# TensorE's program written out, and the first tile of a projection taken k by k

## What is computed

```python
def even_layer(h, ...):                     # layer 0
    z = rms_norm(h, pre_g) @ w_in           # 2048 x 6144
    u, pool_gate, q, k, v, attn_gate = jnp.split(z, EVEN_SPLITS, axis=-1)
    d, pool_state = multiscale_pool(u, pool_prev, positions)
    pool_out = grouped_linear(d, pool_w) * pool_scale
    o = diff_attn(rope(q), rope(k), v, lam) # prompt: causal; sample: paged cache
    o = rms_norm(o, subln_g) * (1.0 - LAMBDA_INIT)
    mix = jnp.concatenate([pool_out * silu(pool_gate), o * silu(attn_gate)], -1)
    return h + rms_norm(mix @ w_out, post_g)

def odd_layer(h, s0, ...):                  # layer 1
    z = rms_norm(h, pre_g) @ w_in           # 2048 x 6160
    q, k, v, gate, lr = jnp.split(z, ODD_SPLITS, axis=-1)
    g = log_sigmoid(lr @ wa2 + ba) / GLA_TAU
    o, st = gla_scan(q, k, v, g, s0, chunk) # gated linear attention, 4 heads
    o = rms_norm(o, norm_g) * silu(gate)
    return h + rms_norm(o @ w_out, post_g)
```

## Time and profile before

| | us |
|---|---|
| median of 3 runs | 2238.65 |
| lowest and highest run | 2235.77, 2240.67 |
| the profiled execution | 2231.26 |
| its span, from first to last instruction | 2229.1 |
| mean granted clock of TensorE | 0.949 of 2.4 GHz |

### The profile page before, as it was taken

One profiled execution on the slowest core, in us unless ns is written; L12 is line 12 of the kernel. 1 busy time (PEld: TensorE's weight loads), 2 busy tenths in 40 slices (PEclk: granted clock), 3 DMA queues, 4 the chain that ended last, 5 costly groups with the idle time before them and its releaser, 6 DMA issues.

```text
span 2229.1 us, 39746 instructions
## 1 busy us (share of the span) xinstructions
PE 2036.3 (91%) x15037; PEld 1873.0 (84%) x15037; DVE 813.0 (36%) x1402; ACT 644.5 (29%) x1158; POOL 816.2 (37%) x369
## 2 busy tenths in 40 slices
PE   4998898889889998899889999999999899969995
PEld 4987898789878887899879878987997799759995
DVE  4355236523652454300261444053315322550004
ACT  5132222222221221322233333333224232442122
POOL 1353236232622352645454212421332233144553
PEclk7999999999989999999999999999999899979997
DMA  6444234423442443433234342444244325433322
GB/s 199 150 132 135 79 110 119 133 77 117 124 119 74 120 131 112 136 94 89 69 104 115 114 142 77 114 130 136 68 120 148 113 67 147 146 126 95 94 75 77
DMA packets 357433, 252.49 MB, mean 113 GB/s; under 512 B 15135, under 2 KB 324784, under 8 KB 356720
## 3 DMA queue, kind: packets, MB, share of 16 engines
q1 hardware_dynamic: 316364, 186.75, 29.3%
q10 hardware_dynamic: 40900, 63.41, 8.4%
HBM read 213.61 MB, written 36.96 MB: 112 GB/s over the span
## 4 chain that ended last, share of the span: by engine, by line
PE 70%; issue 10%; POOL 6%; DVE 5%; SPq 3%; DMA 3%; ACT 2%; POOLq 0%; ACTq 0%; DVEq 0%
PE proj L983 57%; PE scratch L983 9%; PE score L983 3%; POOL wlo L554 3%; DMA qb<-q_sample_rows 2%; SPq L466 1%; SPq L458 1%; PE scratch L986 1%; POOL mix L608 1%; POOL kv L575 1%; DVE probw L1494 1%; DVE xlo L1344 1%; DVE ek L1724 1%; POOL mix L623 1%; DMA kv<-in_cache_v 0%
## 5 line engine op out<-in xcount | busy, mean ns | idle before, releaser
L983 PE MATMUL proj<-xhi,wlo 128*128 128x268 f32 x4128 | 1209.5, 293 | 68.7 <-DVE xlo L1342 27.8
L983 PE MATMUL proj<-xhi,whi 128*128 128x268 f32 x4128 | 1196.7, 290 | 11.0 <-issue 11.0
L983 PE MATMUL proj<-xlo,whi 128*128 128x268 f32 x4128 | 1197.6, 290 | 0.0
L554 POOL TENSOR_TENSOR wlo<-wraw,whi 128x1024 fp32r<-128x1024 f32 x258 | 624.1, 2429 | 1055.6 <-ACT whi L634 1055.5
L983 PEld LDWEIGHTS proj<-xhi,wlo 128*128 128x128 f32 x4128 | 793.9, 192 | 108.3 <-issue 90.9
L983 PEld LDWEIGHTS proj<-xlo,whi 128*128 128x128 f32 x4128 | 793.5, 192 | 1.0
L983 PEld LDWEIGHTS proj<-xhi,whi 128*128 128x128 f32 x4128 | 790.6, 192 | 0.0
L634 ACT ACTIVATE whi<-wraw 128x1024 fp32r<-128x1024 f32 x258 | 264.4, 1046 | 481.6 <-PE proj L983 353.0
L1332 DVE TENSOR_TENSOR tz<-proj,rstd 128x536 f32<-128x536 f32 x72 | 51.5, 716 | 390.6 <-PE proj L983 390.1
L1634 DVE TENSOR_SCALAR mix<-proj,cols 128x536 f32 x32 | 24.8, 776 | 348.8 <-ACT te L640 177.8
L575 POOL TENSOR_TENSOR kv<-kv,qb 128x1024 f32<-128x1024 f32 x32 | 78.4, 2455 | 108.5 <-DMA qb<-q_sample_rows 55.4
(11 more groups left out here) (260 smaller groups left out, 1808.1 us busy)
## 6 DMA issues: line engine op xcount, KB each, us to landing
wraw<-in_w_in SPq DMA_DIRECT2D x192, 512.0 KB, 4.0
wraw<-in_w_out SPq DMA_DIRECT2D x64, 512.0 KB, 3.9
kv<-in_cache_k SPq DMA_DIRECT2D x128, 128.0 KB, 2.4
kv<-in_cache_v SPq DMA_DIRECT2D x128, 128.0 KB, 2.5
sst<-in_state_gla ACTq DMA_DIRECT2D x32, 512.0 KB, 5.3
out<-sst ACTq DMA_DIRECT2D x32, 512.0 KB, 3.6
hbuf<-h_residual ACTq DMA_DIRECT2D x2, 4288.0 KB, 14.7
vb<-v_sample_rows ACTq DMA_DIRECT2D x32, 256.0 KB, 5.8
```

Of the source, the lines that this page charges most:

```text
L554: pool.tensor_tensor(wlo[:, slot, :, 0:width], wraw[:, kc, :, 0:width], whi[:, slot, :, 0:width].bitcast(F32), ALU.subtract).then_inc(s_lo, 1)
L983: return pe.matmul(out, lhsT, rhs, start=start, stop=stop, skip_group_check=True)
```

## The change

1. TensorE's three loops become Python loops, so that its program is written out in full, with constants as semaphore targets.
2. The first tile of "in0", "out0" and "out1" is done by a new function, `first_tile`: block by block, both halves of the columns, each block waiting for its own low part. The order of blocks is `X_ORDER`.
3. `lows` of GpSimd is removed, and its semaphore `s_xp`. VectorE makes all 16 lows of each stage in `x_lo`, which takes a stretch of the order; ScalarE's high parts are made in `x_hi`. In the last pair and the last head both are called in pieces between the other work. For that ScalarE's last pair and head, and VectorE's last head, are written out behind loops that are one pass shorter, and `s_mix` is raised once for each block or group that becomes complete.
4. TensorE's waits for the constants (`s_c0`) and the masks (`s_maskr`) move from before the first pair into the jobs that read them.

```diff
+X_ORDER = {"in0": list(range(KT)), "out0": [0, 1, 2, 3, 4, 5, 8, 9, 10, 11, 12, 13, 6, 14, 15, 7],
+           "in1": list(range(KT)), "out1": list(range(KT))}
...
             # GpSimd
-            lows("out0")
...
-            lows("out1")
...
             # ScalarE
+            def x_hi(stage, a, b):
+                for i in range(a, b):
+                    k = X_ORDER[stage][i]
+                    if i == 0:
+                        act.wait_ge(s_tile, (N_OUT0 if stage == "out0" else N_OUT1) + 2)
+                        act.wait_ge(*(free_d.at("pair", "PO11", PAIRS - 2) if stage == "out0" else (s_head, GH - 1)))
+                    if stage == "out0" and k == 6:
+                        act.wait_ge(*free_d.at("pair", "PO01", PAIRS - 1))
+                    if stage == "out0" and k in (14, 7):
+                        act.wait_ge(s_mix, 1 if k == 14 else 2)
+                    if stage == "out1" and k >= 12:
+                        act.wait_ge(s_mix, 3 + k - 12)
+                    act.activation(xhi[:, k, :], mix[:, k, :], ACT.Copy).then_inc(s_xhi, 1)
...
                     if s == 23:
+                        if last:
+                            x_hi("out0", 0, 2)
                         act.wait_ge(*full.at("pair", "SN", g))
...
                         o_rstd(1)
+                if last:
+                    x_hi("out0", 2, 5)
                 sigmoid("pair", "p1", n0 + 11, g)
+            pair(PAIRS - 1, last=True)
+            x_hi("out0", 5, KT)
...
+                if last_head:
+                    x_hi("out1", 0, 5)
                 act.wait_ge(*free_d.at("head", "SO", s))
...
                 sigmoid("head", "g3", n0 + 11, s)
+                if last_head:
+                    x_hi("out1", 5, 7)
...
+            head(GH - 1, last_head=True)
+            x_hi("out1", 7, KT)
...
             # TensorE
-                for s_part, (start, step) in zip((s_x, s_xp), X_LO[stage]):
-                    if step:
-                        pe.wait_ge(s_part, start + step * (kc + 1))
...
+            def first_tile(n, par, stage):
+                pe.wait_ge(s_evac, n + 1)
+                for i, kt in enumerate(X_ORDER[stage]):
+                    kc, k = kt // HC, kt % HC
+                    if k == 0:
+                        pe.wait_ge(s_lo, 2 * n + kc + 3)
+                    pe.wait_ge(s_x, X_SPLIT[stage] + i + 1)
+                    slot = 2 * par + kc
+                    for a in range(2):
+                        x = slice(a * TH, (a + 1) * TH)
+                        out = proj[par][:, a, 0:TH]
+                        matmul(out, wlo[:, slot, k, :], xhi[:, kt, x], start=i == 0, stop=False)
+                        matmul(out, whi[:, slot, k, :], xlo[:, kt, x], start=False, stop=False)
+                        last = matmul(out, whi[:, slot, k, :], xhi[:, kt, x], start=False, stop=i == KT - 1)
+                last.then_inc(s_tile, 1)
...
-            pe.wait_ge(s_c0, 96)
-            pe.wait_ge(s_maskr, 1)
-            with pe.Fori(0, PAIRS) as g:
+            for g in range(PAIRS):
                 pair(g)
...
-                with pe.Fori(0, KT // 2) as i:
-                    for par in range(2):
-                        for kc in range(2):
-                            chunk(2 * i + (n0 + par), (n0 + par) % 2, kc, stage)
+                first_tile(n0, n0 % 2, stage)
+                for n in range(n0 + 1, n0 + KT):
+                    for kc in range(2):
+                        chunk(n, n % 2, kc)
...
-            with pe.Fori(0, GH) as s:
+            for s in range(GH):
                 head(s)
...
             # VectorE
                     if s == 23:
+                        last_pair = g == PAIRS - 1
+                        if last_pair:
+                            x_lo("out0", 0, 2)
                         sample_mix()
+                        if last_pair:
+                            x_lo("out0", 2, 4)
                         mix_head(1)
+                        if last_pair:
+                            dve.sem_inc(s_mix, 1)
                         gate("p1", mix[:, 2 * g + 1, :])
                         pooled_out(1)
...
             dve.sem_inc(s_mix, 1)
-            lows("out0")
+            x_lo("out0", 4, KT)
...
                         dve.tensor_copy(srow, score[0:NB, 0:GV]).then_inc(s_srow, 1)
+                        if last_head:
+                            x_lo("out1", 0, 2)
...
+                if last_head:
+                    x_lo("out1", 2, 5)
                 gate(3)
+                if last_head:
+                    x_lo("out1", 5, 7)
...
                     if v < 3:
                         link(last)
+                        if last_head:
+                            dve.sem_inc(s_mix, 1)
+                            x_lo("out1", 7 + v, 8 + v)
...
             dve.sem_inc(s_mix, 1)
-            lows("out1")
+            x_lo("out1", 10, KT)
```

More of the change, by code:

```diff
@@ L587, in out_proj @@
                 accumulate(r, par, 2 * i + par)
-            def lows(stage):
-                for k in range(1, KT, 2):
-                    pool.wait_ge(s_xhi, X_HI[stage] + k + 1)
-                    pool.tensor_tensor(xlo[:, k, :], mix[:, k, :], xhi[:, k, :].bitcast(F32), ALU.subtract).then_inc(s_xp, 1)
-            lows("out0")
             for par in range(2):
@@ L687, in sigmoid, with pair @@
                 act.activation(te[:], te[:], ACT.Exp, scale=-1.0).then_inc(sigmoid_ready.sem, 1)
-            def pair(g):
+            def x_hi(stage, a, b):
[11 more added lines that the diff above has]
+                    act.activation(xhi[:, k, :], mix[:, k, :], ACT.Copy).then_inc(s_xhi, 1)
+            def pair(g, last=False):
                 n0 = 12 * g
@@ L786, in pair @@
                         o_rstd(1)
+                if last:
+                    x_hi("out0", 2, 5)
                 sigmoid("pair", "p1", n0 + 11, g)
-            with act.Fori(0, PAIRS) as g:
+            with act.Fori(0, PAIRS - 1) as g:
                 chain.enter(g, PAIR_LINKS_ACT)
                 pair(g)
-                chain.leave(PAIRS)
+                chain.leave(PAIRS - 1)
+            pair(PAIRS - 1, last=True)
+            x_hi("out0", 5, KT)
             for s_out, n in ((s_kout, 32), (s_qk, 96), (s_vout[0], 48), (s_vout[1], 48), (s_uout, 32)):
                 act.wait_ge(s_out, n * PAIRS + 1)
-            def mix_hi(phase):
-                act.wait_ge(s_tile, (N_OUT0 if phase == 0 else N_OUT1) + 2)
-                early = ((2 * PAIRS - 2, free_d.at("pair", "PO11", PAIRS - 2)), (4 * GH - 4, (s_head, GH - 1)))[phase]
-                act.wait_ge(*early[1])
-                for k in range(KT):
-                    if k == early[0]:
-                        act.wait_ge(s_mix, phase + 1)
-                    act.activation(xhi[:, k, :], mix[:, k, :], ACT.Copy).then_inc(s_xhi, 1)
             def out_proj(r, n0, i, par, last=False, narrow=False):
@@ L841, in _, with head @@
             act.wait_ge(s_hst, 16 + 16 * KT)
-            def head(s):
+            def head(s, last_head=False):
                 n0 = N_HEAD + 12 * s
@@ L958, in head @@
                 act.activation(r, r, ACT.Exp, scale=-0.5).then_inc(ro_ready.sem, 1)
-            with act.Fori(0, GH) as s:
+            with act.Fori(0, GH - 1) as s:
                 chain.enter(s, HEAD_LINKS_ACT)
                 head(s)
-                chain.leave(GH)
+                chain.leave(GH - 1)
+            head(GH - 1, last_head=True)
+            x_hi("out1", 7, KT)
             act.wait_ge(s_gout, 16 * GH + 1)
@@ L986, in transpose, with chunk @@
                 return pe.transpose(out, x, ident[0:x.shape[0], 0:x.shape[0]])
-            def chunk(n, par, kc, stage):
+            def chunk(n, par, kc):
                 if kc == 0:
@@ L1335, in evac, with x_lo @@
                 dve.wait_ge(s_evac, n + 3)
-            def lows(stage, scale_col=None):
-                for k in range(0, KT, 2 if scale_col is None else 1):
-                    dve.wait_ge(s_xhi, X_HI[stage] + k + 1)
+            def x_lo(stage, a, b, scale_col=None):
+                for i in range(a, b):
+                    k = X_ORDER[stage][i]
+                    dve.wait_ge(s_xhi, X_SPLIT[stage] + i + 1)
                     if scale_col is None:
@@ L1822, in head @@
                         link(last)
+                        if last_head:
+                            dve.sem_inc(s_mix, 1)
+                            x_lo("out1", 7 + v, 8 + v)
                 last.then_inc(s_head, 1)
                 dve.wait_ge(s_head, s + 1)
-            with dve.Fori(0, GH) as s:
+            with dve.Fori(0, GH - 1) as s:
                 chain.enter(s, HEAD_LINKS)
                 head(s)
-                chain.leave(GH)
+                chain.leave(GH - 1)
+            head(GH - 1, last_head=True)
             dve.sem_inc(s_mix, 1)
-            lows("out1")
+            x_lo("out1", 10, KT)
             out_stage(3, N_OUT1, POST1)
```

31 lines of the change are left out of this document (14 added, 17 removed).

## The result

| us | before | after |
|---|---|---|
| median of the runs timed side by side (4 and 4) | 2237.31 | 2157.57 |
| lowest and highest | 2235.77, 2240.67 | 2155.8, 2161.22 |
| profiled execution, span | 2231.26, 2229.1 | 2158.41, 2156.6 |

The ratio is 0.9644, 95% interval 0.9626 to 0.9662: 79.7 us, or 3.6%, faster. The forecast was 2175, 17.4 us too high, and the range ended 2.4 us above the result.

What follows compares the result with a forecast made beforehand. TensorE, busy 91% of the span, was taken as the bound, through its waits and slow clock. Gains 9.5 + 36.6 + 5.0 + 12.4 = 63.5 us took the profiled 2231.26 to 2167.8, for the median 2175; range 2160 to 2203.

Steps and rivals of the forecast that it cites:

- Part 1: TensorE's pair and head edges: loops written out, no jump waits for missing code; gain 36.6 us, bounds 24 and 39.6.
- rival 2: At the loop edges TensorE waits for something the profile does not show, not code, so they stay: 2212 us, 6%.
- Part 2: Start of layer 0: first tile goes step by step behind VectorE's lows; gain 9.5 us, bounds 8.0 and 10.4.
- Part 3: Output projection of layer 0: lows by VectorE alone, two stalls from GpSimd charged; gain 5.0 us, bounds 2.7 and 8.4.
- Part 4: Output projection of layer 1: without GpSimd's lows, two stalls charged, the tile ends earlier; gain 12.4 us, bounds 10.0 and 16.6.
- Rival 1: TensorE's written-out program: code arrives late also where nothing jumps, making it slower, some 2435 us; 4%.
- Rival 3: Pairs take their gain back by waiting longer for cache values by DMA: gain 27.6 us, 2211 us; 7%.
- Rival 4: First tiles, done step by step with holes, keep the clock low throughout: gain 54 us, 2185 us; 13%.

## Why the prediction was wrong, step by step

The four terms give 64.3 us in the profile where 63.5 were forecast. That they come this near is partly luck: they are off by -2.0, +3.9, +1.8 and -2.9, which cancel. The miss of 17.4 lies almost all beside them: in a base that was too high, and in stretches that the sum put at nothing.

**The base (7.2 us of the miss).** The sum of 63.5 us was made against the profiled execution, 2231.26, and gave 2167.8; 7.2 us were then added because the median of three runs lay 7.4 higher. The changed kernel's profiled execution lies 0.8 above its own median, so nothing was to be added; these 0.8, the 0.8 by which the four terms give more than the sum, and 0.4 outside the spans are the rest of the miss. Before's median also moved from 2233.35 to 2237.31 over five sets of runs: 7.4 was partly the chance of three.

**The untouched stretches (8.2 us).** I counted nothing for the rest of pairs and heads; there the profile of after is 7.3 us shorter, and 0.9 elsewhere. They move by steps of about 1.6 us, some 15 matmuls at the low clock (0.1 us more each): in the heads the two profiles of before differ by 3.1 us. Over all profiles shown here, seven with the loops of before (it twice, and its five edits but the written-out one) have 751.9 to 761.0 us in the pairs and 731.1 to 737.5 in the heads, the seven without loops and with the first tiles changed 749.3 to 755.3 and 728.8 to 732.2. The means differ by 2.5 and 3.3. So more than half of the 7.3 may belong to the change; by what, is open. Cheaper waits do not show (the loops put back, above), and no run was made for anything else.

**Part 1 (36.6; 40.5 and, alone, 42.0).** That code is missing at the jumps was right, and rival 2, that something else is waited for, falls: the jumps themselves are recorded with 3.4 to 4.9 us, and the gaps go with them. Wrong were two things. The heads' 3.0 us that I took off for the clock were really to be had: 27.1 for the gaps and 12.5 for the clock, 39.6, are nearly the 40.5 measured. And "a jump costs only where its body is long" is half of it. The long body explains the first gap. The second, five matmuls on, is there because the target stood fourteen instructions ahead of the end of a piece of 256: the shift by sixteen removes it, one of half a piece too, one of two pieces does not. The sum came out near because it took both gaps from the rows. A body of 768 matmuls and as many weight loads (the longer output projection) turns without a gap; one of 1446 and as many (a head) does not.

The Trainium skill (Runtime: NRT & Kernel Launch, "Instruction fetch mechanics") says that a taken branch whose target is outside the fetched window forces a fetch of the target's piece, and gives 256 instructions a piece. The single gaps of 0.96 to 3.26 us and the count of 256 agree; that the second gap is the fetch of the next piece is what the shifts point to, and no row names it.

**Part 2 (9.5; 7.5).** The mechanism held, the wait behind tile 0 too (2.7 forecast, 3.06). GpSimd's first weight low began at 43.37 and not 42.20, since the lows began 0.6 later and took 0.6 longer; the clock fell in that wait: the 48 matmuls behind it take 7.70 us, where 48 in an unbroken run take 5.94. 7.5 lies below my bound of 8.0. No run separates the k by k order from the moved wait for the masks.

**Part 3 (5.0; 6.8).** The two stalls that I charged did not come: the twelve lows kept VectorE, and GpSimd's first operation became longer. The bound without stalls (8.4) would have been right but for a slow start, 2.48 us of wait and 15 matmuls at the low clock.

**Part 4 (12.4; 9.5).** The stalls came here, 8.19 us for six lows as summed (4.1 + 4.2 = 8.3), and the norms ran at 0.77 and 0.72 again. Not summed were the slow clock behind three small waits, and a slower second tile (0.8); the lower bound of 10.0 is nearly it.

Of the rule in part 3 the runs show one more side. The Trainium skill (SBUF — State Buffer, "Who interferes with whom") has one of the two engines locked out for a whole instruction; the trace agrees in both stages, but which one pays differs: GpSimd with 7.09 and 6.97 us for two operations in "out0", VectorE with 8.19 for six lows in "out1", and with 14.41 for sixteen there in the kernel before with VectorE alone. I had charged VectorE both times.

**The rivals.** Rival 1, code late everywhere, fell: 119 pieces and no gap. Rival 3 fell: the pairs keep their gain (23.8 us at their edges), and the cache waits are within the scatter of the kernel before. Rival 4 came in small: 12 to 17 slow matmuls at a time, not the whole tile.

**The range** took in the costs of the terms, but its fast end, 2160, was set from 2164 (all high bounds from the median); from the profiled execution the same bounds give 2156.3. A base and untouched stretches that scatter by several us each belonged in it.

## What to carry to other kernels

Where a long hardware loop shows two gaps a few instructions apart at its head, look at the row of the jump itself and at where it lands before writing it out: a few idle instructions ahead of the loop can be worth half as much, and an edit elsewhere that shifts the program can give or take as much by chance. An operation that locks out another engine is not made cheaper by moving it along that engine's busy run; hold it until the run is over, if its result has the time. Make the sum and the answer against the same base, and give stretches that an edit does not touch their own scatter.

## What was not expected of the hardware

Four small matmuls without use made this program 26.5 us faster (0.9883 [0.9846, 0.992]), by moving the targets of six jumps off the end of a fetched piece. A jump back over a pair or a head took 3.3 to 5.0 us in these runs, one over 768 matmuls 0.23. When VectorE's lows followed one another closely, GpSimd's weight low took 4.74 us in place of 2.4 and VectorE lost nothing ("out0"); in "out1" six such lows lost 4.3 us to the same two operations. What decides between the two is not settled by these runs.
